# Probabilities times values of eight samples: by head in four strips of the array instead of all heads at once

## Chip, cores and metric

The kernel runs on one core of one Trainium2 chip. The metric is the device time in microseconds (us) of one execution, lower is better. Before the change the median of three runs is 1550.62 us (1548.86 to 1551.59).

## What is computed

One step of a hybrid decoder layer, for a prompt of 256 tokens and for 8 samples of one token each, with the same weights in float32. Cut to what matters here, the samples' attention:

```python
def dilated_sample(q, k, v, kv_buf, dil):      # for each of three head groups g, 4 heads x 128 each
    kv_all = jnp.concatenate([kv_buf, jnp.stack([k, v], axis=2).astype(kv_buf.dtype)], axis=1)
    kv_g = jnp.take(kv_all, jnp.maximum(idx, 0), axis=1)
    sc = jnp.einsum('bshd,bsjhd->bshj', q, kv_g[:, :, :, 0], preferred_element_type=jnp.float32) * ATT_SCALE
    ...
    p = jnp.exp(sc - m[..., None])
    den = p.sum(axis=-1)
    num = jnp.einsum('bshj,bsjhd->bshd', p.astype(v.dtype), kv_g[:, :, :, 1], preferred_element_type=jnp.float32)
...
def merge_groups(outs, dtype):                 # softmax weights over the three groups
    out = (wts[..., None] * nums).sum(axis=0) / (wts * dens).sum(axis=0)[..., None]
...
# the layer round it: one wide projection, a short convolution, attention, two gates, w_out, a ConvFFN
x = x + (jax.nn.sigmoid(gate_a) * branch_a + jax.nn.sigmoid(gate_b) * branch_b) @ w_out
```

The three groups of a head are merged by their softmax denominators, which is one softmax over the 211 keys of all three groups together (128 + 64 + 16 cached and 3 new ones). The kernel does it that way. The change touches the product of these probabilities with the values, `num`.

## The kernel before

All activations lie with features on the partitions and the 264 tokens (256 prompt, 8 samples) on the free axis. The program is written out by hand for each engine, and semaphores alone set the order. Nearly all the time goes into weight matmuls: weights come in chunks of 256 x 512 (512 KB) by SyncE's DMA queue into `raw`, a ring of four slots. ScalarE copies a chunk to `w_hi` (L356), rounded to float32r, VectorE makes the rest `w_lo` by subtraction (L554), and TensorE does three matmuls with 264 moving columns for each block of 128 x 128: hi by hi, lo by hi, hi by lo (L923 to L925, function `chunk`), 24 for a chunk. It accumulates over chunks in four banks, `acc`. ScalarE and VectorE may work at most four chunks ahead of TensorE, since a slot comes free only when TensorE has used it (`slots_free`).

The phases in order are qkv, ucb (projections of the convolution, with the prompt's attention between its chunks), gate_a, conv_out, gate_b, attn_out, w_out, then the FFN in two halves, each with its up projections (ffn_a, ffn_b) and its down projection (down_a, down_b). Most phases are hardware loops on each engine, whose bodies are fetched again or kept as code.

The samples' attention lies between these phases. During gate_a VectorE computes the scores; GpSimd's queue brings keys, queries and values. After gate_a TensorE turns the scores so that the 32 pairs of sample and head are rows, VectorE and ScalarE do the softmax, and before conv_out's last group TensorE turns the probabilities back: keys on the partitions, 32 columns in the order sample, head. ScalarE copies them into `pt_a` (128 keys) and `pt_b` (83 keys) (L478). These tiles are zero elsewhere and hold, for each sample b, 32 columns of which the four at 4b to 4b+3 are filled. After conv_out come the 16 matmuls of L1062: for each sample and each part of the keys, 32 columns of probabilities are loaded as weights, and the 512 columns of the sample's values (4 heads x 128) move. The sum is 32 rows (sample, head) by 512 columns, in which a row's own head is one quarter. VectorE multiplies by `own_heads`, a mask (L778), and adds the four quarters (L782) into `srows`, of 32 rows by 128. Before the last group of gate_b TensorE turns `srows` (L1068), and VectorE puts the result into `att_hi` and `att_lo` for attn_out.

Of the kernel before, what the change touches and what calls it, by code (L numbers as in the profile page):

```python
# [26 lines left out]
ALU = mybir.AluOpType  # L27
ACT = mybir.ActivationFunctionType
AX_X = mybir.AxisListType.X

P = 128
# [3 lines left out]
HEADS = 4  # L35
HEAD_DIM = 128
# [3 lines left out]
ATT_W = HEADS * HEAD_DIM  # L40
SEQ = 256
BATCH = 8
# [33 lines left out]
ROWS_A = SAMPLE_ROWS[0]  # L76
ROW_G2, ROW_OWN = SAMPLE_ROWS[1], SAMPLE_ROWS[1] + SAMPLE_ROWS[2]
ROWS_B = ROW_OWN + NG
SAMPLE_KEYS = ROWS_A + ROWS_B

# [18 lines left out]
def trunk_program(nc, x_fm, w_in, w_conv_out, w_attn_out, w_out, w_ffn_in, w_ffn_down, params, rope_tab,  # L99
                  masks, own_heads_in, ident_in, st_mix_in, st_ffn_in, caches, q_new, kv_new,  # L100
                  y_out, p_kv, s_kv, conv_state_out, ffn_state_out):
    with ExitStack() as ctx:
        def sem(name):
            return ctx.enter_context(nc.semaphore(name))
# [6 lines left out]
        def place(name, shape, dt=F32, at=None):  # L111
            off = cursor[0] if at is None else at
            n = size[dt] * int(np.prod(shape[1:]))
            t = nc.alloc_sbuf_tensor_at(name, list(shape), dt, offset=off)
            if at is None:
                cursor[0] = off + -(-n // 32) * 32
            return t
# [14 lines left out]
        ident = place("ident", [P, P])  # L132
        ones = place("ones", [P, P])
        st_at = cursor[0]
        st_mix = place("st_mix", [P, 2, CT, BATCH])
# [8 lines left out]
        own_heads = place("own_heads", [BATCH * HEADS, HEADS])  # L144
# [42 lines left out]
        pt_a = place("pt_a", [ROWS_A, BATCH * (HEADS * BATCH + HEADS)])  # L187
        pt_b = place("pt_b", [ROWS_B, BATCH * (HEADS * BATCH + HEADS)])
        sall = place("sall", [BATCH * HEADS, HEADS, HEAD_DIM], at=st_at)
        srows = place("srows", [BATCH * HEADS, HEAD_DIM], at=st_at + 4 * ATT_W)  # L190
# [56 lines left out]
        own_heads_landed, pt_zeroed, picked, srows_ready, sturned_back = (  # L247
            sem("own_heads_landed"), sem("pt_zeroed"), sem("picked"), sem("srows_ready"), sem("sturned_back"))
# [102 lines left out]
        def _(act):  # L351
# [125 lines left out]
            for out, rows, col in ((pt_a, ROWS_A, 512), (pt_b, ROWS_B, 544)):  # L477
                act.activation(out[:, :].rearrange("p (b c) -> p b c", b=BATCH)[:, :, 0:HEADS],  # L478
                               side[0:rows, col:col + BATCH * HEADS].rearrange("p (b h) -> p b h", b=BATCH),
                               ACT.Copy).then_inc(spt_ready, 1)  # L480
# [69 lines left out]
        def _(dve):  # L550
# [212 lines left out]
            with fetched_loop(mybir.EngineType.DVE, 0, 4) as i:  # L763
# [3 lines left out]
                def take_a(m):  # L767
# [7 lines left out]
            dve.wait_ge(own_heads_landed, 16)  # L775
            dve.wait_ge(base_ready, 2)
            dve.wait_ge(shead_done, 1)
            dve.tensor_tensor(sall[:, :, :], side[0:BATCH * HEADS, 1024:1024 + ATT_W].rearrange("p (h d) -> p h d", h=HEADS),  # L778
                              own_heads[:, :].unsqueeze(2).to_broadcast([BATCH * HEADS, HEADS, HEAD_DIM]),
                              ALU.mult).then_inc(picked, 1)  # L780
            dve.wait_ge(picked, 1)
            dve.tensor_reduce(srows[:, :], sall[:, :, :].rearrange("p h d -> p d h"), AX_X, ALU.add).then_inc(srows_ready, 1)  # L782
# [7 lines left out]
            sout = side[:, 0:HEADS * BATCH].rearrange("p (b h) -> p h b", h=HEADS)  # L790
# [114 lines left out]
        def _(pe):  # L905
# [147 lines left out]
            nbh = BATCH * HEADS  # L1053
# [6 lines left out]
            for b in range(BATCH):  # L1060
                for n, (pt, v) in enumerate(((pt_a, v_a), (pt_b, v_b))):
                    mm = pe.matmul(side[0:nbh, 1024:1024 + ATT_W], pt[:, nbh * b:nbh * (b + 1)], v[:, b, :],  # L1062
                                   start=b + n == 0, stop=b + n == BATCH)
# [4 lines left out]
            pe.transpose(side[:, 0:nbh], srows[:, :], ident[0:nbh, 0:nbh]).then_inc(sturned_back, 1)  # L1068
# [38 lines left out]
        def _(pool):  # L1107
# [5 lines left out]
            pool.dma_start(own_heads[:, :], own_heads_in).then_inc(own_heads_landed, 16)  # L1113
# [201 lines left out]
```

## Time and profile before

| what | value |
|---|---|
| median of three runs | 1550.62 us |
| the profiled execution: its time, its span | 1554.01 us, 1552.4 us |
| mean granted TensorE clock | 0.994 |
| TensorE matmuls busy | 1522.6 us (98%) |
| TensorE weight loads busy | 1506.3 us (97%) |
| VectorE busy | 894.8 us (58%) |
| ScalarE busy | 692.9 us (45%) |
| GpSimd busy | 75.4 us (5%) |
| data moved by DMA | 307.77 MB, mean 198 GB/s |

The span goes from the first to the last instruction of one execution. PE is TensorE's matmuls, PEld its weight loads (which overlap them), DVE is VectorE, ACT ScalarE, POOL GpSimd, SP SyncE. A matmul's end is modelled: rows overlap, and what counts is the distance of two starts. "Issue" is a wait for nothing that the profile shows.

### The profile page before, as it was taken

The numbers are of one execution on the slowest core, as the hardware profiler recorded it, in microseconds if no ns is written. First come the engines' busy times: TensorE is split into PE (matmuls) and PEld (weight loads), VectorE is DVE, ScalarE is ACT, GpSimd is POOL, SyncE is SP. The second block draws the span as 40 slices with busy tenths as digits, with TensorE's granted clock in tenths as the row PEclk, the third lists the DMA queues.
The fourth block names the chain that finished last, engine by engine and source line by source line (L and its number), as shares of the span: only waits on it lengthen the run. The fifth ranks groups of instructions, "written<-read, shape, count | busy, mean of one in ns | idle before, by whom it ended". The sixth has DMA issues, their size and how long they took to land.

```text
span 1552.4 us, 32031 instructions
## 1 busy us (share of the span) xinstructions
PE 1522.6 (98%) x12354; PEld 1506.3 (97%) x12354; DVE 894.8 (58%) x1057; ACT 692.9 (45%) x761; POOL 75.4 (5%) x145
## 2 busy tenths in 40 slices
PE   8999999999988999999999999999999999999997
PEld 8999999999988889999999999999999999999996
DVE  8646555756656434676665656654444656556554
ACT  7444444434444334444454444443333444444452
POOL 2000001001230000010000000000000000000000
PEclk9999999999999999999999999999999999999998
DMA  8867676556897636555577777775555666666552
GB/s 274 274 184 247 180 225 184 159 151 197 261 240 207 203 125 201 170 171 181 173 253 237 230 220 235 248 242 170 178 180 175 175 189 179 174 187 191 185 178 97
DMA packets 145139, 307.77 MB, mean 198 GB/s; under 512 B 10144, under 2 KB 10272, under 8 KB 144560
## 3 DMA queue, kind: packets, MB, share of 16 engines
q1 hardware_dynamic: 139120, 268.73, 56.3%
q0 software_dynamic: 5952, 38.12, 7.6%
q8 instruction: 46, 0.75, 0.2%
q14 instruction: 21, 0.17, 0.0%
HBM read 301.39 MB, written 26.38 MB: 211 GB/s over the span
## 4 chain that ended last, share of the span: by engine, by line
PE 94%; DVE 2%; DMA 2%; issue 1%; ACT 1%; SPq 0%; DVEq 0%; ACTq 0%
PE acc L923 31%; PE acc L924 30%; PE acc L925 30%; DMA raw<-w_in 2%; DVE w_lo L554 1%; PE side L1062 1%; ACT w_hi L356 1%; PE side L1016 1%; PE side L995 1%; DVE yg L900 0%; PE side L1007 0%; ACT sq L392 0%; DVE tf L809 0%; PE side L982 0%; DVE tf L813 0%
## 5 line engine op out<-in xcount | busy, mean ns | idle before, releaser
L554 DVE TENSOR_TENSOR w_lo<-raw,w_hi 128x1024 fp32r<-128x1024 f32 x503 | 616.7, 1235 | 541.6 <-ACT w_hi L356 539.4
L356 ACT ACTIVATE w_hi<-raw 128x1024 fp32r<-128x1024 f32 x503 | 529.4, 1058 | 735.6 <-PE acc L925 672.7
L923 PE MATMUL acc<-h_hi,w_hi 128*128 128x264 f32 x2872 | 822.9, 287 | 6.5 <-DVE gate_a L731 3.7
L925 PE MATMUL acc<-h_hi,w_lo 128*128 128x264 f32 x2872 | 817.0, 284 | 0.5 <-issue 0.5
L924 PE MATMUL acc<-h_lo,w_hi 128*128 128x264 f32 x2872 | 817.3, 285 | 0.0
L923 PEld LDWEIGHTS acc<-h_hi,w_hi 128*128 128x128 f32 x2872 | 540.5, 188 | 9.3 <-DVE gate_a L731 4.3
L925 PEld LDWEIGHTS acc<-h_hi,w_lo 128*128 128x128 f32 x2872 | 540.7, 188 | 0.8 <-issue 0.8
L924 PEld LDWEIGHTS acc<-h_lo,w_hi 128*128 128x128 f32 x2872 | 540.7, 188 | 0.1
L923 PE MATMUL acc<-f_hi,w_hi 128*128 128x264 f32 x704 | 201.1, 286 | 2.8 <-issue 2.8
L925 PE MATMUL acc<-f_hi,w_lo 128*128 128x264 f32 x704 | 201.0, 286 | 0.0
L924 PE MATMUL acc<-f_lo,w_hi 128*128 128x264 f32 x704 | 200.5, 285 | 0.0
L923 PEld LDWEIGHTS acc<-f_hi,w_hi 128*128 128x128 f32 x704 | 133.8, 190 | 3.0 <-issue 3.0
L924 PEld LDWEIGHTS acc<-f_lo,w_hi 128*128 128x128 f32 x704 | 133.1, 189 | 0.0
L925 PEld LDWEIGHTS acc<-f_hi,w_lo 128*128 128x128 f32 x704 | 132.9, 189 | 0.0
L923 PE MATMUL acc<-t_hi,w_hi 128*128 128x264 f32 x256 | 72.9, 285 | 0.9 <-DVE tf L809 0.9
L925 PE MATMUL acc<-t_hi,w_lo 128*128 128x264 f32 x256 | 72.8, 284 | 0.0
L924 PE MATMUL acc<-t_lo,w_hi 128*128 128x264 f32 x256 | 72.6, 284 | 0.0
L923 PEld LDWEIGHTS acc<-t_hi,w_hi 128*128 128x128 f32 x256 | 48.4, 189 | 1.1 <-DVE tf L809 1.1
L924 PEld LDWEIGHTS acc<-t_lo,w_hi 128*128 128x128 f32 x256 | 48.1, 188 | 0.0
L925 PEld LDWEIGHTS acc<-t_hi,w_lo 128*128 128x128 f32 x256 | 48.1, 188 | 0.0
L924 PE MATMUL acc<-ab_lo,w_hi 128*128 128x264 f32 x128 | 37.0, 289 | 2.7 <-issue 2.7
L923 PE MATMUL acc<-ab_hi,w_hi 128*128 128x264 f32 x128 | 37.4, 293 | 0.5 <-DVE gate_a L731 0.4
(188 smaller groups left out, 851.0 us busy)
## 6 DMA issues: line engine op xcount, KB each, us to landing
raw<-w_in SPq DMA_DIRECT2D x183, 512.0 KB, 3.8
raw<-w_ffn_in SPq DMA_DIRECT2D x176, 512.0 KB, 4.3
raw<-w_ffn_down SPq DMA_DIRECT2D x88, 512.0 KB, 3.9
raw<-w_out SPq DMA_DIRECT2D x32, 512.0 KB, 4.6
s_kv<-cache POOLq DMA_DIRECT2D x16, 1020.0 KB, 9.0
raw<-w_conv_out SPq DMA_DIRECT2D x16, 512.0 KB, 4.2
raw<-w_attn_out SPq DMA_DIRECT2D x8, 512.0 KB, 3.9
s_kv<-cache POOLq DMA_DIRECT2D x8, 508.0 KB, 4.9
```

Source lines behind the costliest of these rows:

```text
L356: act.activation(w_hi[:, s % RING], raw[:, s % RING], ACT.Copy).then_inc(hi_ready, 1)
L554: dve.tensor_tensor(w_lo[:, s % RING], raw[:, s % RING], w_hi[:, s % RING].bitcast(F32), ALU.subtract).then_inc(lo_ready, 1)
L923: pe.matmul(out, w_hi[:, slot, k, cols], backwards(m_hi[:, kt + k, :]), start=first and k == 0, stop=False)
L924: pe.matmul(out, w_hi[:, slot, k, cols], backwards(m_lo[:, kt + k, :]), start=False, stop=False)
L925: mm = pe.matmul(out, w_lo[:, slot, k, cols], backwards(m_hi[:, kt + k, :]), start=False, stop=last and k == 1)
L995: mm = pe.matmul(side[:, SCORES + n * g:SCORES + n * (g + 1)], qkv[:, 12 * g + h, P * qt:P * (qt + 1)], qkv[:, 12 * g + 4 + h, 0:n], start ...
L1016: mm = pe.matmul(side[:, HEAD_OUT:HEAD_OUT + P], vtok[:, kb, (g * HEADS + h) * HEAD_DIM:(g * HEADS + h + 1) * HEAD_DIM], prob_t[:, P * b:P ...
L1062: mm = pe.matmul(side[0:nbh, 1024:1024 + ATT_W], pt[:, nbh * b:nbh * (b + 1)], v[:, b, :], start=b + n == 0, stop=b + n == BATCH)
```

## The change

The probabilities are laid out by head: `pt_a[:, h, ...]` holds for head h, for each sample, a block of 32 columns with one filled column. Each of the 16 matmuls becomes four, one for each head, with 32 loaded columns and 128 moving columns. The output of head h goes to the partitions 32h to 32h+31, and so to the columns 32h to 32h+31 of the array. Rows of another head are never computed, so mask and sum fall away: VectorE copies 128 x 128 out of PSUM, of which 8 rows in each 32 carry data. The transpose takes 128 rows, and reading picks the 32 columns wanted. The mask's tile and DMA go; the zeroed tiles grow from 288 to 1056 columns.

```diff
-        pt_a = place("pt_a", [ROWS_A, BATCH * (HEADS * BATCH + HEADS)])
-        pt_b = place("pt_b", [ROWS_B, BATCH * (HEADS * BATCH + HEADS)])
-        sall = place("sall", [BATCH * HEADS, HEADS, HEAD_DIM], at=st_at)
-        srows = place("srows", [BATCH * HEADS, HEAD_DIM], at=st_at + 4 * ATT_W)
+        pt_a = place("pt_a", [ROWS_A, HEADS, BATCH * (STRIP + 1)])
+        pt_b = place("pt_b", [ROWS_B, HEADS, BATCH * (STRIP + 1)])
+        srows = place("srows", [P, HEAD_DIM], at=st_at)
...
-                act.activation(out[:, :].rearrange("p (b c) -> p b c", b=BATCH)[:, :, 0:HEADS],
-                               side[0:rows, col:col + BATCH * HEADS].rearrange("p (b h) -> p b h", b=BATCH),
+                act.activation(out[:, :, :].rearrange("p h (b c) -> p h b c", b=BATCH)[:, :, :, 0],
+                               side[0:rows, col:col + BATCH * HEADS].rearrange("p (b h) -> p h b", b=BATCH),
...
-            dve.wait_ge(own_heads_landed, 16)
             dve.wait_ge(base_ready, 2)
             dve.wait_ge(shead_done, 1)
-            dve.tensor_tensor(sall[:, :, :], side[0:BATCH * HEADS, 1024:1024 + ATT_W].rearrange("p (h d) -> p h d", h=HEADS),
-                              own_heads[:, :].unsqueeze(2).to_broadcast([BATCH * HEADS, HEADS, HEAD_DIM]),
-                              ALU.mult).then_inc(picked, 1)
-            dve.wait_ge(picked, 1)
-            dve.tensor_reduce(srows[:, :], sall[:, :, :].rearrange("p h d -> p d h"), AX_X, ALU.add).then_inc(srows_ready, 1)
+            dve.tensor_copy(srows[:, :], side[:, 1024:1024 + HEAD_DIM]).then_inc(srows_ready, 1)
...
-                    mm = pe.matmul(side[0:nbh, 1024:1024 + ATT_W], pt[:, nbh * b:nbh * (b + 1)], v[:, b, :],
-                                   start=b + n == 0, stop=b + n == BATCH)
+                    for h in range(HEADS):
+                        mm = pe.matmul(side[STRIP * h:STRIP * (h + 1), 1024:1024 + HEAD_DIM],
+                                       pt[:, h, STRIP * b:STRIP * (b + 1)], v[:, b, HEAD_DIM * h:HEAD_DIM * (h + 1)],
+                                       start=b + n == 0, stop=b + n == BATCH)
...
-            pe.transpose(side[:, 0:nbh], srows[:, :], ident[0:nbh, 0:nbh]).then_inc(sturned_back, 1)
+            pe.transpose(side[:, 0:P], srows[:, :], ident[:, :]).then_inc(sturned_back, 1)
```

On TensorE, behind the last three matmuls of conv_out, stood this before (`side` is the PSUM tile of the attention, the names behind the arrow are what is read, then the output's size):

```order
2788 L923 MATMUL acc<-ab_hi,w_hi 128x264
2789 L924 MATMUL acc<-ab_lo,w_hi 128x264
2790 L925 MATMUL acc<-ab_hi,w_lo 128x264
2791 L1062 MATMUL side<-v_a,pt_a 32x512
2792 L1062 MATMUL side<-v_b,pt_b 32x512
2793 L1062 MATMUL side<-v_a,pt_a 32x512
```

and this stands there now:

```order
2788 L917 MATMUL acc<-ab_hi,w_hi 128x264
2789 L918 MATMUL acc<-ab_lo,w_hi 128x264
2790 L919 MATMUL acc<-ab_hi,w_lo 128x264
2791 L1057 MATMUL side<-v_a,pt_a 32x128 x4
2792 L1057 MATMUL side<-v_b,pt_b 32x128 x4
2793 L1057 MATMUL side<-v_a,pt_a 32x128 x4
```

Both go on in that pattern to eight rows of each kind; nothing else on TensorE moved against its neighbours, and there are 48 matmuls more.

On VectorE, between the splits for gate_b and the take of gate_b's first tile, stood before:

```order
295 L554 TENSOR_TENSOR w_lo<-raw,w_hi 128x1024 x7
296 L778 TENSOR_TENSOR sall<-side,own_heads 32x512
297 L782 TENSOR_REDUCE srows<-sall 32x128
298 L731 TENSOR_TENSOR gate_b<-acc,r 128x264
299 L554 TENSOR_TENSOR w_lo<-raw,w_hi 128x1024
```

and now:

```order
295 L553 TENSOR_TENSOR w_lo<-raw,w_hi 128x1024 x7
296 L776 COPY srows<-side 128x128
297 L730 TENSOR_TENSOR gate_b<-acc,r 128x264
298 L553 TENSOR_TENSOR w_lo<-raw,w_hi 128x1024
```

Two operations became one at the same place.

## Rows read from the trace of the kernel before

**Rows 1.** The page: span, then busy time of each engine.

```profile
span 1552.4 us, 32031 instructions
PE 1522.6 (98%) x12354; PEld 1506.3 (97%) x12354; DVE 894.8 (58%) x1057; ACT 692.9 (45%) x761; POOL 75.4 (5%) x145
```

**Rows 2.** The page: the chain that ended last, shares by engine.

```profile
PE 94%; DVE 2%; DMA 2%; issue 1%; ACT 1%; SPq 0%; DVEq 0%; ACTq 0%
```

**Rows 3.** Timeline of TensorE's matmuls: start us, us, then the instruction.

```profile
537.09 0.28 PE L925 MATMUL acc<-ab_hi,w_lo 128*128 128x264 f32 x1
537.30 1.04 PE L1062 MATMUL side<-v_a,pt_a 128*32 128x512 f32 x2
538.18 1.02 PE L1062 MATMUL side<-v_b,pt_b 83*32 83x512 f32 x2
539.04 1.02 PE L1062 MATMUL side<-v_a,pt_a 128*32 128x512 f32 x2
...
551.18 0.39 PE L923 MATMUL acc<-h_hi,w_hi 128*128 128x264 f32 x1
```

**Rows 4.** Timeline of VectorE, in brackets the idle time before.

```profile
538.50 1.22 DVE L554 TENSOR_TENSOR w_lo<-raw,w_hi 128x1024 fp32r<-128x1024 f32 x1 [0.54 <-ACT w_hi L356]
555.47 1.23 DVE L554 TENSOR_TENSOR w_lo<-raw,w_hi 128x1024 fp32r<-128x1024 f32 x1 [15.75 <-ACT w_hi L356]
558.41 1.23 DVE L554 TENSOR_TENSOR w_lo<-raw,w_hi 128x1024 fp32r<-128x1024 f32 x1 [1.71 <-ACT w_hi L356]
...
571.20 0.67 DVE L778 TENSOR_TENSOR sall<-side,own_heads 32x512 f32<-32x512 f32 x1
571.91 1.09 DVE L782 TENSOR_REDUCE srows<-sall 32x128 f32<-32x512 f32 x1
```

**Rows 5.** Tile `side`, weight loads: ns min/median/max, first and last start.

```profile
L1062 PEld LDWEIGHTS side<-v_a,pt_a x16: 106/108/110, 537.3 to 549.4; 128*32 128x32 f32 x16
```

**Rows 6.** Timeline of TensorE's matmuls, an attention product of the prompt.

```profile
375.84 1.50 PE L1016 MATMUL side<-prob_t,vtok 128*128 128x128 f32 x12
377.10 0.37 PE L923 MATMUL acc<-h_hi,w_hi 128*128 128x264 f32 x1
```

**Rows 7.** The page: the queue that fetches code, packets and MB.

```profile
q8 instruction: 46, 0.75, 0.2%
```

**Rows 8.** Timelines of TensorE's matmuls round three waits for issue.

```profile
488.39 0.28 PE L923 MATMUL acc<-ab_hi,w_hi 128*128 128x264 f32 x1
491.34 0.29 PE L924 MATMUL acc<-ab_lo,w_hi 128*128 128x264 f32 x1 [2.66 <-issue]
...
1044.38 0.28 PE L925 MATMUL acc<-h_hi,w_lo 128*128 128x264 f32 x1
...
1047.41 0.38 PE L923 MATMUL acc<-f_hi,w_hi 128*128 128x264 f32 x1 [2.75 <-issue]
...
1194.40 0.39 PE L925 MATMUL acc<-h_hi,w_lo 128*128 128x264 f32 x1 [0.54 <-issue]
```

**Rows 9.** Windows: length, PE, PEld, DVE, ACT, POOL busy, PEclk, DMA, GB/s.

```profile
1048.80:1052.30 3.50, 3.50 (x18) 3.50 (x17) 0.17 (x1) 0.36 (x1) 0.00 (x0) 0.51 0.53 159
1052.30:1056.00 3.70, 3.70 (x33) 3.70 (x32) 1.23 (x1) 1.62 (x2) 0.00 (x0) 1.00 0.11 27
```

**Rows 10.** Timeline of TensorE's matmuls, the transpose of the samples' rows.

```profile
621.28 0.24 PE L1068 MATMUL side<-ident,srows 32*128 32x32 f32 x1
621.45 0.39 PE L923 MATMUL acc<-h_hi,w_hi 128*128 128x264 f32 x1
```

**Rows 11.** Timelines of GpSimd, zeroing and the DMAs behind it.

```profile
386.21 0.34 POOL L1202 MEMSET pt_a<- 128x288 f32 x1 [23.92 <-DVE ab_lo L725]
...
386.77 0.76 POOL L1192 DMA_DIRECT2D v_a<-cache  x1
...
404.85 0.74 POOL L1181 DMA_DIRECT2D k_a<-cache  x1 [15.62 <-DVE sc_b L750]
```

**Rows 12.** Tile `side`, VectorE's copy of 128x128: ns min/median/max.

```profile
L694 DVE COPY att_f<-side x8: 280/282/284, 260.2 to 378.3; 128x128 f32<-128x128 f32 x8
```

More of the change, by code:

```diff
@@ L79 @@
 SAMPLE_KEYS = ROWS_A + ROWS_B
+STRIP = P // HEADS
 SCORE, EXP, NORM, TURN, OUT = 5, 6, 7, 9, 11
@@ L99, in trunk_program @@
 def trunk_program(nc, x_fm, w_in, w_conv_out, w_attn_out, w_out, w_ffn_in, w_ffn_down, params, rope_tab,
-                  masks, own_heads_in, ident_in, st_mix_in, st_ffn_in, caches, q_new, kv_new,
+                  masks, ident_in, st_mix_in, st_ffn_in, caches, q_new, kv_new,
                   y_out, p_kv, s_kv, conv_state_out, ffn_state_out):
@@ L143, in trunk_program @@
         sc_b = place("sc_b", [ROWS_B, BATCH * HEADS])
-        own_heads = place("own_heads", [BATCH * HEADS, HEADS])
         small = place("small", [P, 4, 2 * HEADS])
@@ L246, in trunk_program @@
             sem("sprob_ready"), sem("spt_done"), sem("spt_ready"), sem("shead_done"))
-        own_heads_landed, pt_zeroed, picked, srows_ready, sturned_back = (
-            sem("own_heads_landed"), sem("pt_zeroed"), sem("picked"), sem("srows_ready"), sem("sturned_back"))
+        pt_zeroed, srows_ready, sturned_back = (
+            sem("pt_zeroed"), sem("srows_ready"), sem("sturned_back"))
         satt_f, satt_hi, satt_ready = sem("satt_f"), sem("satt_hi"), sem("satt_ready")
@@ L789, in _ @@
             dve.wait_ge(sturned_back, 1)
-            sout = side[:, 0:HEADS * BATCH].rearrange("p (b h) -> p h b", h=HEADS)
+            sout = side[:, 0:P].rearrange("p (h c) -> p h c", h=HEADS)[:, :, 0:BATCH]
             satt = att_tmp[:, :].rearrange("p (h b) -> p h b", h=HEADS)
@@ L1112, in _ @@
             pool.dma_start(ident[:, :], ident_in).then_inc(ident_landed, 16)
-            pool.dma_start(own_heads[:, :], own_heads_in).then_inc(own_heads_landed, 16)
             pool.dma_start(mask[:, :], masks).then_inc(mask_landed, 16)
@@ L1272 @@
         "rope_tab": rope_table(), "masks": mask_table(), "ident": np.eye(P, dtype=np.float32),
-        "own_heads": np.tile(np.eye(HEADS, dtype=np.float32), (BATCH, 1)),
         "st_mix": per_feature(a["state_conv_mix"][0]).transpose(0, 2, 3, 1),
@@ L1294 @@
     trunk_program(nc, aps["x_fm"], aps["w_in"], aps["w_conv_out"], aps["w_attn_out"], aps["w_out"], aps["w_ffn_in"],
-                  aps["w_ffn_down"], aps["params"], aps["rope_tab"], aps["masks"], aps["own_heads"], aps["ident"], aps["st_mix"],
+                  aps["w_ffn_down"], aps["params"], aps["rope_tab"], aps["masks"], aps["ident"], aps["st_mix"],
                   aps["st_ffn"], [aps[f"cache{g}"] for g in range(NG)], q_new, kv_new,
```

## Prediction

> **What bounds the kernel now.** I read the page first: TensorE is busy for 1522.6 of 1552.4 us, VectorE for 58% of them [rows 1], and the chain that ended last is TensorE for 94% [rows 2]. So a microsecond taken from TensorE's queue comes off the end, as long as the weights for what follows lie ready. The timeline of TensorE round the samples' values [rows 3] shows the place of the change: the last matmul of conv_out starts at 537.09, then the 16 matmuls of L1062 run as pairs of passes (two records each, since f32 goes through the array twice), and the first matmul of gate_b starts at 551.18. From 537.30 that is 13.88 us. Two neighbouring rows start 0.86 us apart, so a pass of 512 columns takes 0.43 us. The load is 32 columns wide, so three quarters of the array's columns stand idle, and of the 512 results in each output row only the 128 of the row's own head are kept.
>
> VectorE's timeline of the same stretch [rows 4] says whether time saved there reaches the end. Its split of weights at 538.50 is the last for a long while: all four slots of the ring are then full, and the next split starts at 555.47 after 15.75 us without work. The feeders were ready at 539.7. If the block ended anywhere after that, gate_b would start with a full ring, four chunks of 2.9 us each (the distance of the splits at 555.47 and 558.41), or 0.12 for each of a chunk's 24 matmuls.
>
> **The matmuls of the values.** Removed: 32 passes of 512 columns, 13.88 us. Added: 64 matmuls of 128 columns, 128 passes, each with a load of 32 columns. Nothing in the trace shows two matmuls in different strips of the array at once; the price of a pass of 128 f32 columns is shown: L1016 has 12 of them in 1.50 us with the last one's 0.275 in it, so they start 0.111 us apart [rows 6]. The loads of 32 columns take 0.108 us as records [rows 5], but lie under the running pass: passes start 0.43 apart with a load in each, and 0.111 apart in L1016 with loads four times as wide.
>
> The bounds follow. With one pass at a time: 128 x 0.111 = 14.2 us, 0.3 more than now. With all four strips at work all the time: 14.2 / 4 = 3.6 us, 10.3 less. Between them lies what the order of the program allows. It issues strip 0's two passes, then strip 1's two, and so on. The two passes of one matmul share a strip and follow each other. If matmuls start in the program's order, strip 1's first pass can start beside strip 0's second, but its own second must wait 0.111 us, and then strip 2's first goes with it. So one matmul of 128 columns is done each 0.111 us: 64 x 0.111 = 7.1 us, 6.8 less than now. This I take: it needs strips that run side by side and nothing else, and it is twice rather than four times as fast because of the two passes.
>
> The Trainium skill's page "TensorE: Matmul & The Clock Gate" (Part 3: Packing small matmuls) gives strips that run side by side, matmuls that start strictly in order, and 2.38 times the speed for three column strips; by that factor the block would be an estimated 6.0 us. The same part says that a weight load overlaps a running matmul only in another row group, and here every strip uses all rows; the loads of [rows 5] lie under matmuls of the same row groups, so this trace does not agree. By the page's rule the loads would be bare, which is the rival on the slow side below. No run here shows the column strips yet.
>
> **The transpose back** handles 128 instead of 32 rows. Now it costs 0.17 us to the next matmul [rows 10]; with 128 rows a further 0.1 at most, from the 0.111 of a pass. +0.1.
>
> **What lies beside other work.** VectorE's two operations, 0.67 and 1.09 us [rows 4], become one copy of 128x128 out of PSUM, which elsewhere takes 0.28 [rows 12]. They run at 571 between the split of the last weights and the take of gate_b's first tile, while TensorE works on; no wait of TensorE is seen there. So nothing is gained; without that cover it would be 1.5 us. The transpose that waits for these rows starts at 621.28 [rows 10], and they are there by 573. GpSimd clears 1056 instead of 288 columns twice, 0.34 us each now [rows 11]; by the ratio of the sizes at most 1.25 each, so the first values' DMAs start up to 1.8 us later than 386.77. GpSimd then waits until 404.85 for scores anyway, and the values are wanted at 537. Nothing. ScalarE's two copies have the same size, with another step. One small DMA less on GpSimd, at 17.6 us where nothing waits for it.
>
> **The code itself.** TensorE's program grows by 48 matmuls of four instructions (two loads, two passes), 192 instructions in all. The instruction queue moved 46 packets, 0.75 MB, so 16 KB each [rows 7]. I counted about 12,160 instructions for TensorE in the built program of before; 0.75 MB over them is 62 bytes each, so I take 64 and 256 to a packet. Then everything behind the block moves by 0.75 packet. That matters because TensorE idles at loop ends where the next packet is not there [rows 8]: 2.75 us at 1047.41, where the loop of the first FFN half ends and down_a begins, 0.54 at 1194.40, and 2.66 at 491.34, all put down to "issue". Counted so, with the start shifted by 56 instructions to let the first of them fall on a boundary, the loop's end stands at 36.00 packets, and the one at 1194.40 comes 90 instructions behind down_a, where the trace has it too. After the stall at 1047.41 the granted clock falls to 0.51, half of 2.4 GHz, for the 3.5 us from 1048.8; 18 matmuls run in it, where the next 3.7 us hold 33 [rows 9]. Those 18 want 2.0 us at full clock, so 1.5 are lost.
>
> After the change the ends of the loops stand at 25.93 (gate_b), 30.55 (w_out), 36.75 (FFN, first half), 41.40 (down_a), 44.52 (FFN, second half). The stall at 1047.41 goes with its slow clock, -2.75 - 1.5, and the one at 1194.40, -0.5. But gate_b's loop now ends 19 instructions ahead of a boundary, some 10 matmuls of 0.12 us, so a stall of 2.75 - 1.1 = 1.6 us can appear there, near 615. Sum -3.2 us. The stall at 491.34 lies ahead of the change and stays. Bounds: -4.8 if gate_b's end gets by, and nothing or +1 if my count of positions is off and another loop's end falls on a boundary (each such costs up to 2.75 + 1.5).
>
> **Sum**: -6.8 + 0.1 - 3.2 = -9.9 us. The profiled execution took 1554.0 with a span of 1552.4; the median of the runs is 1550.6. The differences carry over: 1544.1 for a profiled one, 1540.7 for the median of the runs.
>
> **The rivals.** (a) All strips run side by side, 3.6 us for the block, because the array does not hold strip 2 back behind strip 1's second pass: 1540.7 - 3.5 = 1537.2. For it: matmuls can start 0.03 us apart, as L923 behind L1016 nearly shows by its long first record [rows 6]. Against it: the order of the two passes. Up to four times is also what the skill's page "TensorEngine Tiling (Array Packing)" (Theoretical Speedup) allows. (b) The strips don't run side by side for f32, so the change doesn't do what it says: 14.2 us, 1540.7 + 7.1 = 1547.8 with the code's share, 1551.0 without. For it: no row of this trace has two matmuls at once in steady state; a shape of 32 columns runs no faster now than one of 128. (c) Slower: a load cannot hide when the strip changes, so each of the 128 passes pays 0.108 + 0.111: 28.0 us, 14.1 more, 1540.7 + 20.9 = 1561.6. It decides from a bare 0.02 us per load on, which eats the code's share (128 x 0.025 = 3.2). Against it: [rows 5] have loads under matmuls, pass behind pass. (d) The code's share fails to come: each of the above 3.2 us later, so 1543.9 for my forecast.
>
> **How the numbers follow.** Two strips at a time 0.48, rival (a) 0.17, (b) 0.28, (c) 0.07. The code's share comes in two of three cases whichever holds. A measurement of this kernel can tell about 0.2%, 3.1 us, from no change: faster is below 1547.5. The first two cases are faster, and a third of (b), where the code's stalls come out a little better: 0.48 + 0.17 + 0.10 = 0.75. The same: the rest of (b), 0.17. Slower: (c) and a new stall over (b), 0.08. Range: from (a) at 1537.2 to (b) with the code's share at 1547.8, so 1537 to 1548; left out are (c), most of (b) without the code's share, and a little of (a) where gate_b's end gets by.
>
> **What would show it.** The stretch from the first row of the values to gate_b's first matmul should be 7.1 us, with passes that overlap: two starts each 0.111 us. 14 us would be (b), under 5 (a), over 17 (c). VectorE's idle time behind the fourth split should be 9 us instead of 15.75, ended by ScalarE and not by a DMA. There should be no wait for issue at the start of down_a and no half clock there, and one of up to 1.6 us after gate_b's loop. The prediction is wrong if passes of different strips are spaced as those of one, or if a stall of 2.7 us with a slow clock comes up at another loop.

## The result and the profile after

The changed kernel takes 1544.52 us (median, 1541.08 to 1546.52) where the kernel before, run beside it, takes 1553.55 (1548.86 to 1556.77). The ratio is 0.9936 with a 95% interval of 0.9924 to 0.9949, so 9.9 us are gained, with 1.9 on either side. (The two medians are 9.0 apart.) That is the size that was forecast, but its two large terms were both off, in opposite directions, so the agreement is luck. The time itself lies inside the forecast's 1537 to 1548, 3.8 above its 1540.7: that figure started from a median of 1550.62 in three runs, where the eight runs beside the changed kernel give 1553.55.

The page of the changed kernel gives the span, the busy time of each engine, and the queue that fetches code; it answers to [rows 1] and [rows 7].

```profile
span 1544.1 us, 32221 instructions
PE 1514.0 (98%) x12450; PEld 1508.2 (98%) x12450; DVE 893.1 (58%) x1056; ACT 693.0 (45%) x761; POOL 76.3 (5%) x144
q8 instruction: 47, 0.77, 0.2%
```

The bound is the same as before, TensorE. Its span is 8.3 us shorter than in [rows 1] in these two executions (1545.92 and 1554.01 us as wholes), and its busy time 8.6.

**The block of the values.** The timeline of TensorE's matmuls in the changed kernel (start us, us, then the instruction, x8 being eight passes in one row) answers to [rows 3]. The row behind it is from the chain that ended last, with start and length of the whole block.

```profile
535.30 0.28 PE L919 MATMUL acc<-ab_hi,w_lo 128*128 128x264 f32 x1
535.52 0.43 PE L1057 MATMUL side<-v_a,pt_a 128*32 128x128 f32 x8
535.76 0.41 PE L1057 MATMUL side<-v_b,pt_b 83*32 83x128 f32 x8
535.98 0.40 PE L1057 MATMUL side<-v_a,pt_a 128*32 128x128 f32 x8
...
538.84 0.40 PE L1057 MATMUL side<-v_b,pt_b 83*32 83x128 f32 x8
539.17 0.39 PE L917 MATMUL acc<-h_hi,w_hi 128*128 128x264 f32 x1
```

```profile
535.59 3.66 PE side L1057 x128
```

Eight passes (four heads, two passes each) begin every 0.22 us, and the next eight start while the last still run: a row is 0.40 us long, 0.22 behind the one ahead of it. In the chain 128 passes take 3.66 us, 10.2 less than the 13.88 of before. A single pass still lasts as long as one of this size does alone; tile `side` (ns min/median/max, first and last start):

```profile
L1057 PEld LDWEIGHTS side<-v_a,pt_a x64: 106/108/111, 535.5 to 538.6; 128*32 128x32 f32 x64
L1057 PE MATMUL side<-v_a,pt_a x64: 270/272/297, 535.5 to 538.8; 128*32 128x128 f32 x64
```

**VectorE behind it.** Its timeline answers to [rows 4]; the idle time ahead of an instruction stands in brackets. The split after the ring's fourth slot comes after 5.52 us of idle time instead of 15.75, and ScalarE's `w_hi` ends it, so gate_b starts with a full ring here too. The multiplication and the sum of the mask are now one copy of 0.28 us.

```profile
536.72 1.23 DVE L553 TENSOR_TENSOR w_lo<-raw,w_hi 128x1024 fp32r<-128x1024 f32 x1 [0.54 <-ACT w_hi L355]
543.46 1.23 DVE L553 TENSOR_TENSOR w_lo<-raw,w_hi 128x1024 fp32r<-128x1024 f32 x1 [5.52 <-ACT w_hi L355]
...
559.20 0.28 DVE L776 COPY srows<-side 128x128 f32<-128x128 f32 x1
```

**The waits for code.** The timeline of TensorE round its waits for issue of 1 us and more answers to [rows 8]. The windows behind it (length, then PE, PEld, DVE, ACT, POOL busy with instructions, granted clock, DMA share, GB/s) answer to [rows 9].

```profile
491.06 0.28 PE L918 MATMUL acc<-ab_lo,w_hi 128*128 128x264 f32 x1 [1.00 <-issue]
...
610.02 0.28 PE L917 MATMUL acc<-h_hi,w_hi 128*128 128x264 f32 x1
612.37 0.49 PE L918 MATMUL acc<-h_lo,w_hi 128*128 128x264 f32 x1 [2.07 <-issue]
...
1043.12 0.59 PE L917 MATMUL acc<-f_hi,w_hi 128*128 128x264 f32 x1 [3.46 <-issue]
```

```profile
609.50:612.40 2.90, 0.83 (x8) 0.62 (x6) 0.43 (x2) 2.26 (x2) 0.00 (x0) 1.00 0.66 188
612.50:616.00 3.50, 3.50 (x17) 3.50 (x18) 1.23 (x1) 0.95 (x2) 0.00 (x0) 0.51 0.05 7
616.00:619.50 3.50, 3.50 (x31) 3.50 (x31) 1.23 (x1) 1.29 (x2) 0.00 (x0) 1.00 0.48 148
1039.60:1043.10 3.50, 0.06 (x1) 0.00 (x0) 2.24 (x2) 0.78 (x1) 0.00 (x0) 0.93 0.36 112
1043.10:1046.00 2.90, 2.88 (x13) 2.88 (x14) 0.00 (x0) 0.00 (x0) 0.00 (x0) 0.50 0.77 278
```

There is a new wait of 2.07 us behind gate_b's loop, and the one at down_a is still there, longer, 3.46 instead of 2.75, and some 50 instructions further into down_a. Behind both the granted clock is 0.51 and 0.50, the lower of the two levels (1.2 GHz): 17 matmuls run in the 3.5 us from 612.50, 31 in the 3.5 us behind them. At 0.12 us from start to start those 17 want 2.0 us, so such a stretch costs about 1.5.

**The sum of the two executions.** Distances of matmul starts across each place, from the timelines, before and after: the block -10.2; behind gate_b's loop 2.35 where 0.12 is usual, +2.2; at down_a 3.03 and 3.74, +0.7; the wait of [rows 8] at 1194.40 is gone, -0.7; one more stretch at half clock, +1.5; from the matmul ahead of the transpose back to the one behind it 0.39 and 0.15, -0.24; ahead of the change, in conv_out, 2.94 and 1.29, -1.65. Together -8.4, of the 8.3 seen. The code's share is thus +3.7 us behind the change and +2.1 with conv_out's, where -3.2 was forecast.

### The profile page after: what moved, and what is told of

Read it like the earlier page. It is cut to its first block, busy times and chain, and to the rows that moved or that the text cites. A ratio compares the mean times of both kernels' runs of the same rounds, so it can differ in the third digit from the quotient of the medians.

```text
span 1544.1 us, 32221 instructions
## 1 busy us (share of the span) xinstructions
PE 1514.0 (98%) x12450; PEld 1508.2 (98%) x12450; DVE 893.1 (58%) x1056; ACT 693.0 (45%) x761; POOL 76.3 (5%) x144
## 4 chain that ended last, share of the span: by engine, by line
PE 95%; DVE 2%; DMA 1%; issue 1%; ACT 1%; SPq 0%; DVEq 0%; ACTq 0%
PE acc L917 31%; PE acc L918 31%; PE acc L919 31%; DMA raw<-w_in 1%; DVE w_lo L553 1%; PE side L1010 1%; PE side L989 1%; ACT w_hi L355 0%; DVE yg L894 0%; PE side L1001 0%; PE side L1057 0%; DVE gate_a L730 0%; DVE tf L803 0%; PE side L976 0%; DVE tf L807 0%
```

## The experiments

### How wide the array works: one strip, two strips, half the columns

All three are the changed kernel, and the number of instructions stays. The first two have other places for the block's output: in the first all heads go to strip 0, in the second heads 0 and 2 to strip 0 and heads 1 and 3 to strip 1. VectorE still reads by strips, so these two leave out the right attention output of most heads; the work on TensorE is the same.

```diff
-  mm = pe.matmul(side[STRIP * h:STRIP * (h + 1), 1024:1024 + HEAD_DIM],
+  at, to = STRIP * (h % 1), 1024 + HEAD_DIM * (h // 1)     # one strip; two strips: h % 2 and h // 2
+  mm = pe.matmul(side[at:at + STRIP, to:to + HEAD_DIM],
...
-                 start=b + n == 0, stop=b + n == BATCH)
+                 start=b + n == 0 and h < 1, stop=b + n == BATCH, skip_group_check=True)     # two strips: h < 2
```

> The changed kernel with the outputs of all four heads in the same 32 columns of the array (partitions 0 to 31) and side by side in PSUM's columns; same number, size and order of matmuls. The samples' attention output is wrong for three heads of four, since VectorE still reads by strips. Theory 1 (the block took 3.67 us after the change because four strips run side by side): with one strip the 128 passes go one behind the other, 0.107 to 0.111 us each, block 13.7 to 14.2 us, the kernel 10.2 us slower than the changed one, so within 2 us of the time before. Rival (short matmuls of 128 columns are cheap by themselves, by the way the loads overlap): block stays at 3.7 us.

> The same with heads 0 and 2 in one strip, 1 and 3 in a second one (three of four heads' outputs then read wrongly or not at all). Theory 1 (each strip takes its own pass at full length, and consecutive matmuls overlap where the strips differ): two strips hold twice one strip's rate, block 6.8 to 7.1 us. My forecast's rule (matmuls start in order and a matmul's two passes share a strip, so at most two run side by side) is dead for four strips, where it said 7.1 and 3.67 was measured; if what limits is how many passes may be in flight, two strips would give more than 7.1, up to 14.

The third keeps the strips and lets 64 columns of the values move instead of 128, so it leaves out half of each head's output.

```diff
-  mm = pe.matmul(side[STRIP * h:STRIP * (h + 1), 1024:1024 + HEAD_DIM],
+  mm = pe.matmul(side[STRIP * h:STRIP * (h + 1), 1024:1024 + HEAD_DIM // 2],
-  pt[:, h, STRIP * b:STRIP * (b + 1)], v[:, b, HEAD_DIM * h:HEAD_DIM * (h + 1)],
+  pt[:, h, STRIP * b:STRIP * (b + 1)], v[:, b, HEAD_DIM * h:HEAD_DIM * h + HEAD_DIM // 2],
```

> The changed kernel with 64 instead of 128 moving columns in each of the 64 matmuls (half of the values of each head are left out, so the samples' attention is wrong). In the changed kernel 128 passes start 0.0275 us apart. If the array sets that (a pass of 128 columns lasts 0.107 us in each of four strips), half the columns give 0.013 to 0.014 us, block 1.9 us. If the issue of load and matmul sets it (0.0275 for a pair), or the load of 32 columns (by the difference of the loads' rows, 0.188 for 128 and 0.108 for 32 columns, 0.027), the block stays at 3.6 us.

The chain's piece for the block, in one strip, in two strips, and with half the columns (start us, us):

```profile
533.30 14.12 PE side L1058 x128
```

```profile
534.24 7.14 PE side L1058 x128
```

```profile
534.61 1.95 PE side L1057 x128
```

One strip takes 14.12 us, 0.110 for each of 128 passes; two take 7.14, half; four take 3.66, a quarter. The whole kernel follows: with one strip 1552.73 us and ratio 0.999 (0.998 to 1.0), no gain; with two, a single run, 1546.25. The time per pass is therefore a pass's own 0.110 us divided by the strips in use. Half the columns halve it again, to 1.95 us (the kernel at 1539.0, one run), so neither the issue of instructions nor the 128 weight loads set the rate: at 1.95 us they pass at one in 0.015 us.

The one-strip kernel also answers the rule on loads that the forecast weighed. Its rows for tile `side`:

```profile
L1058 PEld LDWEIGHTS side<-v_a,pt_a x64: 106/110/112, 533.2 to 546.2; 128*32 128x32 f32 x64
L1058 PE MATMUL side<-v_a,pt_a x64: 270/272/297, 533.2 to 546.3; 128*32 128x128 f32 x64
```

Loads of 110 ns in the same rows and the same strip as the running passes, and a pass each 0.110 us: nothing of them shows. The trace does not agree with the Trainium skill's page "TensorE: Matmul & The Clock Gate" (Part 3: Packing small matmuls) that a load overlaps a matmul only in another row group. The same part also lets a load into a background weight buffer go ahead of running matmuls, and with that the trace agrees. Its 2.38 times for three column strips is 0.79 a strip, under the 0.96 a strip of the 3.86 times of four strips against one here (14.12 / 3.66); "Up to 4x" of the page "TensorEngine Tiling (Array Packing)" (Theoretical Speedup) is what this kernel nearly reaches.

### In what order the strips get work: head by head

The forecast held that starts in the program's order let only two strips work, since a matmul's two passes follow each other in one strip. Here the loop over heads is the outermost, so 32 passes of one strip stand behind each other.

```diff
+            for h in range(HEADS):
                 for b in range(BATCH):
                     for n, (pt, v) in enumerate(((pt_a, v_a), (pt_b, v_b))):
-                        for h in range(HEADS):
```

> The changed kernel with the 64 matmuls of the values in another order: all 16 of head 0, then all 16 of head 1, and so on, so that neighbours share a strip except at three places. The same work and result. If TensorE starts matmuls strictly in the program's order, neighbours cannot run side by side: block 128 x 0.109 = 14.0 us. If each strip has a queue that the sequencer fills ahead, later heads' matmuls start early and the block is under 12 us, towards 3.7.

Timeline of this kernel at its start and round the first change of head, and its chain:

```profile
536.01 0.41 PE L1057 MATMUL side<-v_a,pt_a 128*32 128x128 f32 x2
536.26 0.38 PE L1057 MATMUL side<-v_b,pt_b 83*32 83x128 f32 x2
...
538.90 0.38 PE L1057 MATMUL side<-v_b,pt_b 83*32 83x128 f32 x2
539.12 0.41 PE L1057 MATMUL side<-v_a,pt_a 128*32 128x128 f32 x4
539.34 0.41 PE L1057 MATMUL side<-v_b,pt_b 83*32 83x128 f32 x4
```

```profile
536.08 12.97 PE side L1057 x128
```

12.97 us, 1.15 less than in one strip; the kernel takes 1552.79 (one run). A new row of two passes starts 0.22 us behind the last, as in one strip. Only at the three changes of head do passes overlap. The rows at 539.12 and 539.34 hold four passes each instead of two: the last two passes of head 0 on `v_a` with the first two of head 1, then the same on `v_b`. In the program both passes of head 0 on `v_b` stand ahead of those first two of head 1, so starts do not keep the program's order across strips. Four passes overlap at each change, which saves some 0.4 us each time. So the array takes work past a busy strip, but only a few passes ahead. The expectation's two cases were 14.0 and under 12 towards 3.7; 12.97 is neither, a look ahead that is short. In the changed kernel's order that look ahead is enough: each strip's second pass waits for its first without holding back the strips behind it. This is the step at which the forecast's 7.1 us failed. That the look ahead is a queue of some four passes fits these two orders and was not varied further.

### Whether the position of the code makes the waits

Theory: the waits come where a loop ends near the end of one of the 16 KB packets of code [rows 7], so that a shift of the code alone, without any other work, moves or removes them. The rival: they belong to the loops, or to the DMA traffic of that place.

The first kernel is the one before with empty instructions in conv_out's last group, meant to shift what follows by 192 as the change does. The built program holds only six instructions more than before, where the expectation speaks of 192, so it does not put the code where the changed kernel has it.

```diff
+                    for _ in range(pad // TILES):
+                        pe.nop(nofuse=True)
...
-            run(3 + QUAD0["conv_out"], 3 + GROUP0["conv_out"], N_CONV, ab_hi, ab_lo)
+            run(3 + QUAD0["conv_out"], 3 + GROUP0["conv_out"], N_CONV, ab_hi, ab_lo, pad=48)
```

> The kernel before, with 192 empty instructions spread over TensorE's last group of conv_out, so that its code behind lies where the changed kernel's does; the values' matmuls are those of before. Theory 2 (waits for issue depend on where a loop's end lies in the fetched packets of 256 instructions): the waits sit as after the change, some 2.1 us with half clock behind gate_b's loop and 3.5 us with half clock at the start of down_a, none at the second FFN half; block 13.9 us; time up to 3 us above before. Rival (the waits moved for another reason, such as the time at which the fetch meets other DMAs): waits as before the change, 2.7 us at down_a's start and none at gate_b's end, time as before within 1 us.

It took 1548.27 us (1544.73 to 1550.32) with a ratio of 0.9961 (0.9946 to 0.9975) to before. Six instructions that do nothing go with 6 us less (3.9 to 8.4). All of TensorE's waits for issue, by line (us in total, times, longest):

```profile
PE acc L926 <- issue: 1.7, 1, 1.7
PE acc L925 <- issue: 0.8, 2, 0.5
```

The wait at down_a, its half clock and the one at 1194.40 are gone, and the only long one left is of 1.7 us in conv_out. Neither the expected pattern nor the rival's came. The block is 13.88 us as before.

The second is the kernel before with the head of gate_b's loop at the position in a packet that it has in the changed kernel by the prediction's way of counting, with padding ahead of it.

```diff
-            with fetched_loop(mybir.EngineType.PE, 0, 3) as i:      # gate_b, in the kernel before
+            with fetched_loop(mybir.EngineType.PE, 0, 3, slot=93) as i:
```

> The kernel before, with TensorE's loop of gate_b started at place 93 of a packet of 256 instructions, where by my count it stands in the changed kernel (it stands near 157 now); only unused code is added, and a jump over it. The shifted kernel of before had only 6 of its 192 empty instructions left in the built program, and still lost both waits behind the change. Theory 2 (place of the loops' ends in the packets sets the waits for issue): waits as in the changed kernel, 2.1 us behind gate_b's loop and 3.5 us in down_a's first chunks, each with a stretch at half clock; time about 1 to 4 us above before. Rival (the waits come from the time at which the fetch happens, or from the values' block): waits as before.

The waits of this kernel, in TensorE's timeline:

```profile
619.32 0.39 PE L926 MATMUL acc<-h_hi,w_lo 128*128 128x264 f32 x1 [1.69 <-issue]
...
1047.21 0.39 PE L924 MATMUL acc<-f_hi,w_hi 128*128 128x264 f32 x1 [2.35 <-issue]
```

The kernel before now has the changed kernel's pattern: a wait behind gate_b's loop and one in down_a, here too at down_a's 28th matmul, where the kernel before waited at its first. The time, 1551.25 us and a ratio of 0.9989 (0.997 to 1.0007), did not rise as expected: no stretch at half clock follows the wait behind gate_b, and conv_out's wait is 0.51 here instead of 2.66 [rows 8].

The four kernels with other strips, columns or order say the same from the other side. They have the changed kernel's code layout, while their block takes from 1.95 to 14.12 us, so that all behind it comes earlier or later. All four have the two waits at the very matmuls where the changed kernel has them: the 8th behind gate_b's transpose (starts 1.75 to 2.38 us apart) and the 28th of down_a (2.64 to 3.47). So the place of a wait goes with the code's layout, and not with the time or the block. Its length does not. conv_out's wait stands at its 23rd matmul; in the five kernels of this layout the starts there are 1.29, 3.21 and 3.79 us apart, and in two (one strip, half the columns) there is no wait at all. A wait in conv_out that is shorter or missing in one profile thus proves nothing about a shift.

The third and fourth shift the changed kernel: gate_b's loop to place 163, and gate_a's loop to place 128 (with conv_out and all that follows it).

```diff
-            with fetched_loop(mybir.EngineType.PE, 0, 3) as i:      # gate_b
+            with fetched_loop(mybir.EngineType.PE, 0, 3, slot=163) as i:
```

> The changed kernel with TensorE's loop of gate_b started at place 163 instead of (by my count) 93, where it stood in the kernel before with six more instructions, which had no wait for issue behind the values. Theory 2: no wait for issue behind gate_b's loop and at down_a, which with their half clocks cost the changed kernel 2.35 - 0.12 + 3.74 - 0.12 + twice 1.5 = 8.9 us; time 7 to 9 us below the changed kernel, ratio to before near 0.988. Rival (positions don't matter by themselves): time and waits as the changed kernel, 0.994.

```diff
-            with fetched_loop(mybir.EngineType.PE, 0, 4) as i:      # gate_a
+            with fetched_loop(mybir.EngineType.PE, 0, 4, slot=128) as i:
```

> The changed kernel with TensorE's loop of gate_a started at place 128 of a packet (52 by my count now), which moves all loops behind it: conv_out's loop then lies within one packet, from 22 to 225, and gate_b's loop starts near 169. Theory 2: the wait for issue in conv_out's first chunk (1.3 to 3.2 us in the runs so far) goes as well as the two behind it: 2 to 4 us below the other changed kernel with its gate_b loop at 163, if conv_out's end at 225, 31 instructions ahead of a boundary, costs no wait of its own (up to 1.5 us). Rival: as the changed kernel.

Place 163 gave 1541.21 us (ratio 0.9927, 0.99 to 0.9954). The waits behind gate_b and at down_a are gone, as expected, but not the time: the ratio lies nearer to the rival's 0.994 than to the 0.988 forecast, and its interval holds the changed kernel's 0.9936. The 2.7 left in the first view below is conv_out's, ahead of the change. But TensorE now stands for 3.0 us at the start of down_b, in the second. Place 128 gave 1538.14 (0.99, 0.9877 to 0.9924), 3.1 us under place 163 by the medians, with intervals that overlap: conv_out has no long wait in this profile, and the long one left is at down_b, in the third.

```profile
PE acc L919 <- issue: 2.7, 1, 2.7
PE acc L918 <- issue: 0.2, 1, 0.2
```

```profile
1406.76 0.28 PE L920 MATMUL acc<-f_hi,w_lo 128*128 128x264 f32 x1
1409.77 0.29 PE L918 MATMUL acc<-f_hi,w_hi 128*128 128x264 f32 x1 [2.72 <-DVE w_lo L554]
```

```profile
1408.63 0.39 PE L920 MATMUL acc<-f_hi,w_lo 128*128 128x264 f32 x1 [2.26 <-issue]
```

The profile puts the second down to VectorE's split, of which the one at hand began at 1407.65 and took some 1.2 us, so it was over 0.9 us ahead of the matmul; whether code was late there was not separated. The kernel before with six more instructions has gate_b's loop at 163 by the same count and no wait at down_b, so that place alone does not settle it. A shift of the code alone thus moves the waits from loop end to loop end; each layout tried so far had one of over 1.6 us somewhere.

### Whether the hint on the loops makes them

The long waits always stood behind a loop whose end is followed at once by another loop or by straight code: gate_a to conv_out, gate_b to its last group, ffn_a to down_a, ffn_b to down_b. The loops are opened with a hint that they will jump back. Theory: behind such a loop the next packet is fetched only when the code reaches it. Then loops without the hint should have no such wait at any position. The rival is that the hint pays at each jump back, so that leaving it out costs a wait in each iteration. First, beside the shift of the kernel with place 128, the hint is left out of four of TensorE's loops.

```diff
-            return nc.Fori(start, end, engines=(engine,), hint_back_edge=True)
+            return nc.Fori(start, end, engines=(engine,), hint_back_edge=hint, head_slot=...)
...
+            # conv_out, down_a, ffn_b and down_b: fetched_loop(mybir.EngineType.PE, ..., hint=False)
```

> The changed kernel with gate_a's loop at place 128, and without the prefetch hint of the back edge in the four loops of TensorE that follow another loop at once (conv_out, down_a, ffn_b, down_b). In all runs so far a wait of over 2 us for issue behind gate_b came only where a loop ends close to a packet's end or where a hinted loop follows within a few instructions. Theory 3 (the hint of the next loop stops the fetch of the next packet that a loop's end sets off): the wait of 2.5 us at the second FFN half's end and its half clock go, 3 to 4 us below the kernel with the place alone. Rival (the hint saves a wait at each back edge of these loops): waits of up to 2.5 us at their 9 back edges, up to 20 us more.

Then, in the changed kernel without any shift, out of all loops of TensorE, and the same one line in the kernel before; the third is a repeat of the first beside the second.

```diff
-            return nc.Fori(start, end, engines=(engine,), hint_back_edge=True)
+            return nc.Fori(start, end, engines=(engine,), hint_back_edge=engine != mybir.EngineType.PE)
```

> The changed kernel with no prefetch hint in any of TensorE's loops, everything in its place. Theory 3: no wait of over 2 us at down_a's start (gate_b's end, 19 instructions ahead of a boundary, may keep a part): 4 to 9 us below the changed kernel. Rival: waits at the back edges, up to 2.5 us at 22 of them, up to 55 us more.

> The kernel before, without prefetch hints in TensorE's loops. With no wait for issue in either, the distance to the changed kernel without hints is the values' block alone. Theory 3: the waits of 2.94 us in conv_out, 3.03 at down_a with its half clock and 0.83 go, some 8 us below before, ratio 0.995; and the changed kernel without hints, run beside it, is 10.2 us below this one (13.88 against 3.66 us of block). Rival: the gain from leaving out the hints is the changed kernel's alone, ratio 1.0 here.

> The changed kernel without hints once more, on the same chip as the kernel before without hints: 10.2 us below that one, ratio to before 0.988.

| kernel | median us | range | ratio to before | interval |
|---|---|---|---|---|
| changed | 1544.52 | 1541.08–1546.52 | 0.9936 | 0.9924–0.9949 |
| changed, place 128, four loops without hint | 1533.63 | 1532.21–1537.42 | 0.9878 | 0.9854–0.9901 |
| changed, no hints | 1535.21 | 1531.42–1538.51 | 0.9878 | 0.9847–0.9908 |
| changed, no hints, again | 1534.04 | 1531.58–1534.86 | 0.9875 | 0.9857–0.9894 |
| before, no hints | 1543.02 | 1541.50–1547.37 | 0.9933 | 0.9917–0.9949 |

TensorE's waits for issue, by line, first of the kernel before without hints, then of the changed kernel without hints (the repeat), with two lines of its page:

```profile
PE acc L923 <- issue: 0.5, 1, 0.5
```

```profile
PE acc L917 <- issue: 0.2, 1, 0.2
```

```profile
span 1530.0 us, 32191 instructions
...
PE 1509.3 (99%) x12450; PEld 1504.5 (98%) x12450; DVE 892.6 (58%) x1056; ACT 692.9 (45%) x761; POOL 77.3 (5%) x144
```

Without the hints the long waits are gone in both kernels, and no wait at the jumps back takes their place. Leaving them out takes 30 instructions away (12 where four loops lose theirs), so positions move as well, and no run took the hints out with every position kept. But these are three layouts (before, changed, and changed with place 128, where the other loops keep their hints), and none of their four profiles has a wait for issue over 0.51 us, where all ten profiled kernels with every hint, in six layouts, had one of 1.7 or more. The page's span is 14.1 us under that of the changed kernel, with the same matmuls; in the other profile of the same kernel it is 9.2 under (1534.9). Of these two, the slower has three stretches at half clock behind waits for VectorE, the faster one has a single one, beside one at the end of each. Leaving the hints out is worth 10.4 us in the kernel before (0.0067 of 1554) and 9.0 in the changed one (0.9936 to 0.9878). The kernel with place 128 and four hints less is 4.5 us under the one with all its hints by the medians, 3.4 by the ratios, where 3 to 4 were expected; their intervals overlap. Between the two kernels without hints lies what the change itself does: 0.9933 to 0.9875, 9.0 us, with intervals of 2.5 us or more on each ratio. The block's 10.2, which was expected, lies within that. The changed kernel without hints, at either place, beats both kernels, by 9 us more than the change; the lowest median is 1533.63, and the two layouts cannot be told apart.

On this the Trainium skill's page "Runtime: NRT & Kernel Launch" (Instruction fetch mechanics) says that code comes in 16 KB blocks fetched in sequence, that a boundary is mostly hidden, and that a taken branch out of the fetched window breaks the sequence. With hints the trace does not agree on the middle part, if the waits are for such blocks: near the ends of loops they take up to 3.46 us in the changed kernel. Without them it does, 0.2 and 0.5 us for the longest wait of each kernel.

What stays open: why some places with hinted loops have no wait (down_a in the kernel with six more instructions, ffn_b in the kernel before). Why one place has waits of such different length is open too. The exact rule by which a hinted loop's fetch is late was not found. That the waits go with the hint is seen in three layouts, not shown at kept positions; that the packet's boundary is what they wait for is only argued.

## Why the prediction was right, and where not

**The place of the gain was right.** TensorE's time came off the end, VectorE's and GpSimd's work beside it cost nothing, and the matmuls in different strips run at once.

**The block: the size was off by the step on order.** Forecast 7.1 us, measured 3.66. The step that failed is "If matmuls start in the program's order, strip 1's first pass can start beside strip 0's second, but its own second must wait 0.111 us". Starts do not keep the program's order across strips, as the change of head at 539.12 shows. Two strips in use would take 7.14 us as measured with two, so the arithmetic held. With four, the order of passes holds nothing back, as rival (a) said: mechanism and number (3.6) are that rival's. The kernel with heads one after the other shows that order does count once more than about four passes of a strip stand behind each other.

**Rivals (b) and (c)** are out: one strip is the 14.1 us of (b) and four strips are not that; by (c) the changed kernel's 128 passes, with a change of strip between them, would have taken 28.0 us and not 3.66. (In (c) the load that eats the code's share is 0.025 us, as its product has it, and not 0.02.)

**The code's share: the sign was off.** Forecast -3.2, measured +2.1 in the two profiled executions; by the ratio, -9.9 less the block's -10.2 and the transpose's -0.2 leaves +0.5, give or take 1.9. Its parts: the wait of 0.5 at 1194.40 went, as forecast. The wait behind gate_b's loop came where it was forecast (610 for "near 615"), with 2.07 instead of 1.6, and with a stretch at half clock of 1.5 that the forecast did not price. The wait at down_a did not go but grew by 0.7 and kept its half clock; that is the step that failed, "The stall at 1047.41 goes with its slow clock", 4.25 us by itself. It counted a boundary as dangerous only where it falls on a loop's end, and the changed kernel had its wait some 50 instructions past that end. The bounds (-4.8 to +1) were too narrow on the upper side for the two profiled executions; by the ratio that is not shown. By its own last sign, a stall with a slow clock at another loop, the forecast's account of the code was wrong, although the time came out. The wait in conv_out, 2.66, was to stay and is 1.00; kernels with the same code there have from none to 3.51, so its size could not be forecast from positions.

**The sum** agrees at 9.9 by luck: the block gave 3.4 more than forecast and the transpose 0.3 more, and the code's share 3.7 less by the ratio.

**The rest.** The transpose back costs less, where 0.1 more was allowed: from the matmul ahead of it to the one behind are 0.15 us now (609.06 to 609.21), where 0.39 stood before (621.06 to 621.45). Every profiled kernel with 128 rows has the one figure and every one with 32 the other; why 128 rows turn faster than 32 is open. The forecast read 0.17 as its cost in [rows 10] and left out the distance ahead of it. The rows now, and the one of before that [rows 10] begins behind:

```profile
609.06 0.28 PE L919 MATMUL acc<-h_hi,w_lo 128*128 128x264 f32 x1
609.18 0.27 PE L1064 MATMUL side<-ident,srows 128*128 128x128 f32 x1
609.21 0.37 PE L917 MATMUL acc<-h_hi,w_hi 128*128 128x264 f32 x1
```

```profile
621.06 0.28 PE L925 MATMUL acc<-h_hi,w_lo 128*128 128x264 f32 x1
```

GpSimd's zeroing took 0.98 and 1.00 us, under the 1.25 allowed, and the values' first DMA started at 387.41, 0.64 later than in [rows 11] and not 1.8; nothing waited for it. VectorE was idle for 5.52 us, not 9, which follows from the shorter block, and ScalarE ended it as forecast.

## What to carry to other kernels

A matmul that fills only 32 columns of the array is worth splitting into strips, in an order that goes through the strips in turn: here four strips give almost four times the speed, in the order of one head after the other nearly nothing. Before believing a difference of a few microseconds in a long program with loops, look at the waits for issue and what the granted clock does behind them: 9 to 10 us of this kernel lay in waits that come and go with the code's layout and the loops' hints, and the same place can wait 3.5 us in one profile and not at all in that of another kernel with the same code there. So measure a change in two versions of the code's layout, or with the loops' hints out, before its parts are blamed.

## What the runs showed of the hardware

- Passes of f32 in different strips start at once; four strips give 0.029 us a pass of 128 columns (3.66 / 128), one strip 0.110, and loads of 32 columns in the same rows stay hidden in both.
- TensorE starts work past a busy strip about four passes ahead, out of the program's order: 12.97 us for heads one after the other, 14.12 in one strip, with the overlap in the rows at 539.12 and 539.34.
- Six more instructions in straight code went with 6 us less (3.9 to 8.4), and leaving the hints out of TensorE's loops 9 to 10.
- Five kernels of one code layout have their waits for issue at the same matmuls, with blocks of 1.95 to 14.12 us ahead; at one of these places the starts are between 3.79 us apart and not held up at all.
- Of 16 waits for issue in the profiled kernels that held the starts apart by 2 us or more, 11 were followed by a stretch of 3.4 us at a granted clock of half, or fell into one, which costs up to 1.5 us beyond the wait; five were not, one of them of 3.21 us, while one of 2.06 was. None of the four between 1.2 and 2 us (1.97, 1.84, 1.75 and 1.29) was.
